# A decode step on one core: cached pages loaded four rows to a partition, turned by VectorE, scored in 32x32 array tiles

## The chip, the cores and the metric

The kernel runs on one core of one Trainium2 chip. The metric is the device time of one execution in microseconds (us). TensorE (PE) multiplies matrices, VectorE (DVE) and ScalarE (ACT) work element by element, GpSimd (POOL) and SyncE (SP) mostly issue transfers. Each engine runs its own list of instructions in order, and semaphores tie the lists together. SBUF has 128 partitions; matrix products land in eight PSUM banks of 128 x 512 fp32.

## The reference

Two layers; layer 0 is the one that matters. A prompt of 512 tokens and 8 sequences of 4 new tokens go through multi-head latent attention. Each sequence has 4096 cached positions in 32 pages, found through a page table; a page is 128 rows of 320 fp32 (256 latent, 64 rotary key), 160 KB. For a sequence, with 8 heads x 4 tokens = 32 queries:

```python
q_lat = jnp.einsum('bthd,chd->bthc', q_nope, w_uk)
s_past = (jnp.einsum('bthc,bkc->bhtk', q_lat, c_past).astype(jnp.float32)
          + jnp.einsum('bthr,bkr->bhtk', q_rope, kr_past).astype(jnp.float32)) * MLA_SCALE
...
p = jax.nn.softmax(jnp.concatenate([s_past, s_new], axis=-1), axis=-1).astype(c.dtype)
o_lat = (jnp.einsum('bhtk,bkc->bthc', p[..., :past_len], c_past)
         + jnp.einsum('bhtk,bkc->bthc', p[..., past_len:], c))
```

Then come the up-projection by `w_uv`, the output projection by `mla_wo`, a mixture of experts (32 experts, 6 MB of weights each), and layer 1 (sliding-window attention, experts again). All in fp32.

## The kernel before

The part that changes is the sampled stage of layer 0, from about 216 us (absorbing `w_uk` into the queries) to 405.7 us (the last values). It runs over the sequences b = 0..7, and each sequence in quarters t = 0..3 of 8 pages.

**Pages.** `pages[b % 2]` are two buffers of a whole sequence (40 KB a partition each). Page j of a sequence lies in all 128 partitions, 1280 bytes (one row) in each, at column block j. POOL loads sequences 0 and 1 early (L620 to L631), between 65 and 163 us. From b = 2 on, SP loads quarters 0 and 2 (L449 to L461), POOL quarters 1 and 3 (L635 to L645), each page by one DMA. They wait for the values of sequence b-2, which free the buffer piecewise: `page_mm` counts after i = 1, 3 and 5 of the values' loop, `pv_mm` after its end.

**TensorE** for a quarter (`keys_T`, `scores`): 20 transposes of 128x128 (`flip`, L2021) turn the 8 pages' rows into columns, in PSUM banks 2 to 6. ACT copies banks 2, 4 and 6 to SBUF (through a helper at L752), DVE banks 3 and 5 (L1324). Then 12 products score the keys against the 32 queries: weights of 32 columns, four column tiles of the array at a time, 256 keys each, in banks 0 and 1. A product of fp32 (helper `mm`, L2016) shows as two matmul records, a flip as one.

**The softmax.** DVE takes the maximum over bank 0 (L1329, L1331) and bank 1 (L1336), and L1338 makes the negative scaled maximum (semaphore `nms_ready`). ACT's `weigh` takes the exponentials in two halves (L923, L926) and of the new keys (L928). `weights_T` turns the 128x1024 weights back in 8 + 1 flips; ACT and DVE (L1345, L1347) copy them out. `values` is 33 products with four column tiles in bank 7, whose right-hand sides are the page rows themselves.

The order on TensorE is written out by hand: keys_T(b,0), scores(b-1,3), keys_T(b,1), scores(b,0), weights_T(b-1), values(b-1), keys_T(b,2), scores(b,1), keys_T(b,3), scores(b,2). So the softmax of a sequence runs beside the transposes of the next.

After values(6), SP loads `mla_wo` (L493), 4 MB, which the output projection needs right after values(7). `w_uk` and `w_uv` come as one tensor `wkvb`, loaded at 197.4 us.

## Time and profile before

| | |
|---|---|
| median of three runs | 1846.52 us (1845.17 to 1849.54) |
| span of the profiled execution | 1842.6 us |
| TensorE busy | 1743.9 us (95%) |
| VectorE, ScalarE, GpSimd busy | 602.8, 381.9, 214.1 us |
| values of sequence 0 and 7 start at | 253.79 and 399.96 us |
| one sequence (TensorE busy, VectorE busy) | 21.3 us (20.99, 7.96) |

The profiled execution has no time of its own beside its span; the median of the runs is 3.9 us above the span. "Clock" in a stretch is the granted clock of TensorE as a share of 2.4 GHz, so that 0.50 is 1.2 GHz. A row of the groups gives the line, engine, operation and shape, the count, the busy time, the mean of one in ns, then the idle time just before them and who ended it.

### The profile page before, as it was taken

The numbers are of one execution on the slowest core, as the hardware profiler recorded it, in microseconds if no ns is written. First come the engines' busy times: TensorE is split into PE (matmuls) and PEld (weight loads), VectorE is DVE, ScalarE is ACT, GpSimd is POOL, SyncE is SP. The second block draws the span as 40 slices with busy tenths as digits, with TensorE's granted clock in tenths as the row PEclk, the third lists the DMA queues.
The fourth block names the chain that finished last, engine by engine and source line by source line (L and its number), as shares of the span: only waits on it lengthen the run. The fifth ranks groups of instructions, "written<-read, shape, count | busy, mean of one in ns | idle before, by whom it ended". The sixth has DMA issues, their size and how long they took to land.

```text
span 1842.6 us, 29042 instructions
## 1 busy us (share of the span) xinstructions
PE 1743.9 (95%) x9946; PEld 871.1 (47%) x9947; DVE 602.8 (33%) x1586; ACT 381.9 (21%) x858; POOL 214.1 (12%) x312
## 2 busy tenths in 40 slices
PE   7899899999899999999999899999899999999995
PEld 5466676655544444434344445455444444333342
DVE  2334343331522222222222556764322222212223
ACT  2233344431111111111011224342011111111112
POOL 1231014410001000000010201000000010000010
PEclk9899999999989999999999999999899999999998
DMA  6252137775449999999998800032899999999974
GB/s 181 68 155 88 50 116 237 254 253 208 159 182 404 414 421 417 412 419 419 415 418 350 303 14 1 20 138 85 347 375 412 422 414 418 414 421 408 418 307 151
DMA packets 80624, 511.63 MB, mean 278 GB/s; under 512 B 20917, under 2 KB 39302, under 8 KB 54074
## 3 DMA queue, kind: packets, MB, share of 16 engines
q1 hardware_dynamic: 61962, 461.35, 62.1%
q0 software_dynamic: 18576, 49.16, 8.1%
q8 instruction: 51, 0.84, 0.2%
q14 instruction: 35, 0.29, 0.1%
HBM read 498.07 MB, written 26.52 MB: 285 GB/s over the span
## 4 chain that ended last, share of the span: by engine, by line
PE 75%; DMA 14%; DVE 5%; issue 2%; ACT 2%; DVEq 1%; SPq 0%; POOL 0%; ACTq 0%; POOLq 0%
PE ps L2016 65%; DMA mem<-in_moe_w_up 11%; PE ps L2021 10%; ACT mem L752 1%; DMA mem<-in_x_sample 1%; DMA mem<-in_c_masks 1%; DVE mem L1794 0%; DMA mem<-moe_rows_back 0%; DMA mem<-in_cache_mla 0%; DMA moe_rows_back<-mem 0%; DVE mem L1765 0%; DMA mem<-in_swa_sinks 0%; DVE mem L1336 0%; ACT mem L923 0%; ACT mem L926 0%
## 5 line engine op out<-in xcount | busy, mean ns | idle before, releaser
L2016 PE MATMUL ps<-mem 128*64 128x512 f32 (+14 forms) x7970 | 1510.1, 485 | 62.2 <-DMA mem<-moe_rows_back 14.0
L2016 PEld LDWEIGHTS ps<-mem 128*64 128x64 f32 (+4 forms) x7970 | 641.9, 145 | 837.8 <-issue 747.6
L752 ACT ACTIVATE mem<-ps 128x512 f32<-128x512 f32 (+4 forms) x370 | 205.7, 567 | 621.9 <-PE ps L2016 425.2
L2021 PE MATMUL ps<-mem 128*128 128x128 f32 (+1 forms) x1976 | 274.8, 280 | 28.9 <-DMA mem<-in_x_prompt 6.9
L2021 PEld LDWEIGHTS ps<-mem 128*128 128x128 f32 (+1 forms) x1976 | 234.2, 171 | 125.0 <-issue 101.7
L1636 DVE TENSOR_TENSOR mem<-mem,ps 64x512 f32<-64x512 f32 x64 | 44.2, 690 | 433.2 <-ACT mem L995 433.2
L692 POOL DMA_INDIRECT moe_rows_back<-mem x64 | 57.3, 896 | 853.5 <-DVE mem L1653 842.6
L995 ACT ACTIVATE mem<-ps 64x512 f32<-64x512 f32 x64 | 37.7, 589 | 557.8 <-PE ps L2016 557.8
L1653 DVE COPY mem<-ps 64x512 f32<-64x512 f32 x64 | 44.4, 693 | 147.2 <-PE ps L2016 147.2
L1324 DVE COPY mem<-ps 128x512 f32<-128x512 f32 x64 | 44.2, 692 | 77.0 <-PE ps L2021 73.0
L644 POOL DMA_DIRECT2D mem<-in_cache_mla x96 | 51.7, 538 | 104.2 <-PE ps L2016 94.2
L1617 DVE COPY mem<-ps 64x512 f32<-64x512 f32 x32 | 22.2, 694 | 89.4 <-PE ps L2016 89.4
L624 POOL DMA_DIRECT2D mem<-in_cache_mla x64 | 34.4, 538 | 114.1 <-issue 114.1
L1062 ACT ACTIVATE mem<-mem 128x256 f32<-128x256 f32 (+1 forms) x64 | 30.3, 474 | 61.6 <-DVEq L1799 61.6
L682 POOL DMA_INDIRECT mem<-moe_rows_in,mem x34 | 33.2, 977 | 79.3 <-issue 79.3
L1794 DVE CUSTOM_DVE_ANT_0 mem<-ps,mem 128x256 f32<-128x256 f32 (+1 forms) x64 | 26.3, 448 | 27.2 <-PE ps L2016 25.1
L1561 DVE TENSOR_TENSOR mem<-mem 128x320 f32<-128x320 f32 x70 | 34.0, 486 | 2.1
L665 POOL DMA_DIRECT2D moe_rows_in<-mem x10 | 5.4, 538 | 237.8 <-DVE mem L1452 237.8
L1720 DVE SCALAR_TENSOR_TENSOR mem<-mem 128x1024 f32<-128x1024 f32 (+1 forms) x16 | 23.1, 1441 | 23.1 <-DMA mem<-moe_rows_back 21.8
L1644 DVE COPY mem<-ps 128x256 f32<-128x256 f32 x64 | 27.2, 425 | 8.1
L867 ACT ACTIVATE mem<-mem 128x128 f32<-128x128 f32 (+3 forms) x32 | 18.0, 561 | 37.8 <-DVEq L1273 37.8
L1622 DVE TENSOR_TENSOR mem<-ps,mem 128x512 f32<-128x512 f32 x32 | 22.1, 692 | 9.8 <-PE ps L2021 9.7
(237 smaller groups left out, 485.2 us busy)
## 6 DMA issues: line engine op xcount, KB each, us to landing
mem<-in_moe_w_gate SPq DMA_DIRECT2D x64, 2048.0 KB, 21.3
mem<-in_moe_w_up SPq DMA_DIRECT2D x64, 2048.0 KB, 27.8
mem<-in_moe_w_down SPq DMA_DIRECT2D x64, 2048.0 KB, 19.4
mem<-in_cache_mla POOLq DMA_DIRECT2D x160, 160.0 KB, 4.4
mem<-in_cache_mla SPq DMA_DIRECT2D x96, 160.0 KB, 5.5
mem<-moe_rows_back SPq DMA_DIRECT2D x8, 1024.0 KB, 8.7
mem<-in_mla_wo SPq DMA_DIRECT2D x1, 4096.0 KB, 14.1
moe_rows_in<-mem POOLq DMA_DIRECT2D x8, 512.0 KB, 3.0
```

What stands on the lines that cost most here:

```text
L624: g.dma_start(pages_flat[par][:, bass.ds(j * ROW, ROW)], a["cache_mla"][0][bass.ds(page, 1)].rearrange("a p c -> p (a c)")).then_inc(sig[f ...
L644: g.dma_start(pages[b % 2][:, j, :], a["cache_mla"][0][bass.ds(at[n], 1)].rearrange("a p c -> p (a c)")).then_inc(sig[f"late_pages{b % 2}" ...
L682: g.indirect_dma_start(out=xe[b][0:BLK, :], out_offset=None, in_=rows_in, in_offset=bass.IndirectOffsetOnAxis(ap=fetch_at[b][0:BLK, 0:1].b ...
L692: g.indirect_dma_start(out=rows_back, out_offset=bass.IndirectOffsetOnAxis(ap=store_at[b][0:BLK, 0:1].bitcast(U32), axis=0), in_=ye[b][0:B ...
L752: return act.activation(out, in_, ACT.Copy)
L995: act.activation(sg[BLK:2 * BLK, :], ps[0:BLK, b, :], ACT.Silu).then_inc(sig["silu_ready"], 1)
L1324: v.tensor_copy(kT[t % 2][:, n], ps[:, bank, :].rearrange("p (g c) -> p g c", g=2)).then_inc(sig[f"tp_ev{bank}"], 1)
L1561: v.tensor_tensor(onehot[b], rankm[:, :, cols(q, 1)].broadcast_to([P, TILES, BLK]), slots.unsqueeze(1).broadcast_to([P, TILES, BLK]), ALU. ...
L1636: v.tensor_tensor(hid[0:BLK, :], sg[BLK:2 * BLK, :], ps[BLK:2 * BLK, b, :], ALU.mult).then_inc(sig["hid_ready"], 1)
L1653: v.tensor_copy(ye[b][0:BLK, FF:D], ps[BLK:2 * BLK, 2 + b, :]).then_inc(sig["y1_ready"], 1)
L2016: return pe.matmul(out, lhsT, rhs, start=start, stop=stop)
L2021: return pe.transpose(out, in_, ident[at:at + n, at:at + n])
```

## The change

**Loads.** A page now goes to 32 partitions: four consecutive rows (5120 B) to a partition. Page j goes to partitions 32*(j%4) and up, at column block j//4 (of four rows' width). The number of DMAs, their issuers and what they wait for stay.

**Transposes.** The 80 flips of a sequence, and their copies, go. VectorE turns the page buffer in 32x32 blocks straight from SBUF to SBUF: four `transpose` of 128 x 2560 a sequence, into `keysT[0]` and `keysT[1]` (one for each half of the sequence). `keysT` is not double-buffered: keys_T(b,0) waits for the first half of the scores of b-1.

**Scores.** Each 32x32 block is a right-hand side for a 32-row array tile. The queries must lie in every group of 32 partitions: ten products with the selector `pick` spread them (`qrep`), once. A half is 10 (j) x 4 (row tiles i, one PSUM bank each) x 4 (column tiles g) products of 32x32 weights with 128 columns, so 320 a sequence.

**Softmax.** One maximum over 4 banks x 256 (L1327); the exponentials read and write in strides that put the weights back into the pages' order. ACT makes all three copies of `weights_T`. `values` is the same but for its indices.

**Order and the rest.** TensorE now runs weights_T(b-1), values(b-1), scores(b,0), scores(b,1). VectorE runs keys_T(b,0), largest(b-1), keys_T(b,1), (b,2), (b,3). `w_uk` and `w_uv` are loaded by two DMAs each, `w_uv` after the last scores; a load of the last expert's down weights waits for `oc_mm`; one POOL load of the norm's gain waits for the last `weights_T`, as the softmax weights now lie in its place. Buffers are placed anew.

```diff
@@ loads (SP; POOL alike)
-                    sp.dma_start(pages[b % 2][:, j, :], a["cache_mla"][0][bass.ds(at[n], 1)].rearrange("a p c -> p (a c)")
+                    sp.dma_start(four_rows(b % 2, j // 4 * 4 * ROW, j % 4), page_rows(at[n])).then_inc(...)
+        def page_rows(page):
+            return a["cache_mla"][0][bass.ds(page, 1)].rearrange("a (p s) c -> p (a s c)", s=4)
+        def four_rows(par, at, i):
+            return pages_flat[par][32 * i:32 * (i + 1), cols(at, 4 * ROW)]
@@ SP, after values(6)
             sp.dma_start(wo_m, a["mla_wo"][0].rearrange("(k p) n -> p k n", p=P)).then_inc(sig["wo_in"], DMA)
+            sp.wait_ge(sig["qk_mm"], happened("qk_mm", 2 * NB))
+            for k in range(2):
+                sp.dma_start(wuv[:, k], wkv_heads[:, k, :, 1, :]).then_inc(sig["wkvb_in"], DMA)
@@ VectorE
+            def keys_T(b, n):
+                if b < 2 and n == 0:
+                    v.wait_ge(sig[f"late_pages{b % 2}"], landed(f"late_pages{b % 2}", PAGES))
+                if b >= 2:
+                    name, before_ = (("pages", 0), ("late_pages", PAGES), ("third_pages", 0), ("fourth_pages", 0))[n]
+                    v.wait_ge(sig[f"{name}{b % 2}"], landed(f"{name}{b % 2}", before_ + QUARTER * (b // 2)))
+                if n % 2 == 0:
+                    v.wait_ge(sig["qk_mm"], happened("qk_mm", max(2 * (b - 1) + n // 2 + 1, 0)))
+                v.transpose(keysT[n // 2][:, n % 2 * QUARTER * ROW:(n % 2 + 1) * QUARTER * ROW],
+                            pages_flat[b % 2][:, n * QUARTER * ROW:(n + 1) * QUARTER * ROW]).then_inc(sig["keysT_ready"], 1)
+            def largest(b):
+                v.wait_ge(sig["qk_mm"], happened("qk_mm", 2 * b + 2))
+                v.tensor_reduce(m_s[:, b:b + 1], ps[:, 0:4, 0:2 * P], XY, ALU.max)
...
+            keys_T(0, 0)
+            keys_T(0, 1)
             for n in range(1, 4, 2):
                 v.wait_ge(sig["wuk_mm"], happened("wuk_mm", n + 1))
...
+            keys_T(0, 2)
+            for n in range(1, 5, 2):
+                v.wait_ge(sig["qrep_mm"], happened("qrep_mm", n + 1))
+                v.tensor_copy(qrep[:, 2 * n:2 * n + 2], ...)
+            keys_T(0, 3)
...
+            for b in range(1, NB):
+                keys_T(b, 0)
+                largest(b - 1)
+                for n in range(1, 4):
+                    keys_T(b, n)
@@ TensorE
+            for j in range(ROW // 32):
+                rows, q = (slice(0, P), qlat[:, j // 4]) if j < 8 else (slice(0, DR), qmix[0:DR])
+                last = mm(ps[:, j // 2, ...], pick[rows, j % 4, :], q.rearrange("p b q -> p (b q)"), True, True)
+            def scores(b, half_):
+                if half_ == 0:
+                    pe.wait_ge(sig["p_s_ready"], happened("p_s_ready", 2 * b))
+                pe.wait_ge(sig["keysT_ready"], happened("keysT_ready", 4 * b + 2 * half_ + 2))
...
+                for j in range(ROW // 32):
+                    for i in range(4):
+                        for g in range(4):
+                            last = mm(ps[g * NS:(g + 1) * NS, i, c0:c0 + P].rearrange("p (m k) -> p m k", m=4),
+                                      qrep[rows, j, b, :], blocks[rows, :, g, 32 * j:32 * (j + 1)], j == 0, j == ROW // 32 - 1)
```

TensorE's list before, from the end of keys_T(2,1) over scores(2,0) to the first flips of weights_T(1):

```order
L2021 MATMUL ps<-mem 128x128 [waits tp_ev6]
L2021 MATMUL ps<-mem 128x128 x3
L2016 MATMUL ps<-mem 32x256 [waits tp_ev3,tp_ev2,p_s_ready]
L2016 MATMUL ps<-mem 32x256 x3
L2016 MATMUL ps<-mem 32x256 [waits tp_ev5,tp_ev4]
L2016 MATMUL ps<-mem 32x256 x3
L2016 MATMUL ps<-mem 32x256 [waits tp_ev6]
L2016 MATMUL ps<-mem 32x256 x3
L2021 MATMUL ps<-mem 128x128 [waits tp_ev2,p_s_ready]
L2021 MATMUL ps<-mem 128x128 x3
```

and TensorE's list for one whole sequence after (L2013 is `mm` now, L2018 is `flip`):

```order
L2018 MATMUL ps<-mem 128x128 [waits pT_s_ready,p_s_ready]
L2018 MATMUL ps<-mem 128x128 x3
L2018 MATMUL ps<-mem 32x32 [waits pTn_ready]
L2013 MATMUL ps<-mem 32x256 [waits pT_s_ready,o_s_ready]
L2013 MATMUL ps<-mem 32x256 x15
L2013 MATMUL ps<-mem 32x256 [waits pT_s_ready]
L2013 MATMUL ps<-mem 32x256 x15
L2013 MATMUL ps<-mem 32x256 [waits pTn_ready]
L2013 MATMUL ps<-mem 32x128 [waits keysT_ready,p_s_ready]
L2013 MATMUL ps<-mem 32x128 x159
L2013 MATMUL ps<-mem 32x128 [waits keysT_ready]
L2013 MATMUL ps<-mem 32x128 x159
```

The flips and their copies' semaphores (`tp_ev2` to `tp_ev6`) are gone from between the scores, and between scores(b,1) and values(b) nothing else stands any more but the softmax's own flips.

VectorE's list before, keys_T(1,0), the maximum of sequence 0, keys_T(1,1) and a copy of weights_T(0) (the same for later sequences):

```order
L1324 COPY mem<-ps 128x512 [waits tp_mm3,qk_mm]
L1324 COPY mem<-ps 128x512 [waits tp_mm5]
L1336 TENSOR_REDUCE mem<-ps 128x1 [waits qk_mm]
L1338 TENSOR_SCALAR mem<-mem 128x1
L1324 COPY mem<-ps 128x512 [waits tp_mm3,qk_mm]
L1324 COPY mem<-ps 128x512 [waits tp_mm5]
L1345 COPY mem<-ps 128x512 [waits pv_mm,tp_mm3]
```

and after, from keys_T(2,0) with the maximum of sequence 1 behind it:

```order
L1321 STREAM_TRANSPOSE mem<-mem 128x2560 [waits qk_mm,pages0]
L1327 TENSOR_REDUCE mem<-ps 128x1 [waits qk_mm]
L1329 TENSOR_SCALAR mem<-mem 128x1
L1321 STREAM_TRANSPOSE mem<-mem 128x2560 [waits late_pages0]
L1321 STREAM_TRANSPOSE mem<-mem 128x2560 [waits qk_mm,w_a_in]
L1321 STREAM_TRANSPOSE mem<-mem 128x2560 [waits consts_in]
```

The wait for landed pages (`pages0` and so on; `w_a_in` and `consts_in` are the semaphores that the third and the fourth quarter of these buffers share by the table `LATER`) has moved from TensorE to VectorE, and stands ahead of the maximum (L1327) of the sequence before.

## Rows read from the trace of the kernel before

**Rows 1.** Busy time and chain of waits: parts 1 and 4 of the page.
```profile
PE 1743.9 (95%) x9946; PEld 871.1 (47%) x9947; DVE 602.8 (33%) x1586; ACT 381.9 (21%) x858; POOL 214.1 (12%) x312
...
PE 75%; DMA 14%; DVE 5%; issue 2%; ACT 2%; DVEq 1%; SPq 0%; POOL 0%; ACTq 0%; POOLq 0%
```

**Rows 2.** Busy time by stretch: window, length, PE, PEld, DVE, ACT, POOL, clock, DMA share, GB/s.
```profile
228.50:253.80 25.30, 24.99 (x251) 18.86 (x251) 12.11 (x26) 12.72 (x25) 0.00 (x0) 0.92 0.00 1
258.00:279.30 21.30, 20.99 (x252) 14.40 (x253) 7.96 (x14) 9.68 (x20) 8.32 (x17) 1.00 0.75 248
...
399.90:403.30 3.40, 3.34 (x32) 1.80 (x36) 2.73 (x17) 0.00 (x0) 0.00 (x0) 0.51 0.00 0
222.40:228.50 6.10, 3.84 (x17) 3.47 (x16) 2.07 (x7) 1.14 (x3) 0.00 (x0) 0.50 0.01 3
228.50:232.70 4.20, 4.20 (x21) 4.18 (x21) 1.15 (x2) 1.20 (x2) 0.00 (x0) 0.50 0.00 0
```

**Rows 3.** Chain that ends last, start of the sampled stage: start, length, what.
```profile
219.15 4.02 PE ps L2016 x32
...
225.42 3.18 PE ps L2016 x12
228.59 6.53 PE ps L2021 x40
235.12 1.57 PE ps L2016 x24
...
253.79 4.21 PE ps L2016 x66
```

**Rows 4.** Groups by shape, one period, 258 to 279.3 us.
```profile
L2021 PE MATMUL ps<-mem 128*128 128x128 f32 x89 | 11.0, 276 | 0.0
...
L1324 DVE COPY mem<-ps 128x512 f32<-128x512 f32 x8 | 5.5, 692 | 9.4 <-PE ps L2021 8.9
```

**Rows 5.** Timeline, last sequence: start, length, what, idle before and its releaser.
```profile
395.76 0.69 DVE L1336 TENSOR_REDUCE mem<-ps 128x1 f32<-128x512 f32 x1 [2.09 <-PE ps L2016]
...
399.22 0.60 ACT L752 ACTIVATE mem<-ps 128x512 f32<-128x512 f32 x1 [0.16 <-issue]
...
399.96 0.65 PE L2016 MATMUL ps<-mem 128*32 128x256 f32 x4 [0.36 <-ACT mem L752]
```

**Rows 6.** Chain of waits from 400 us.
```profile
399.96 30.22 PE ps L2016 x146
```

**Rows 7.** VectorE groups by shape, longer rows.
```profile
L1452 DVE SCALAR_TENSOR_TENSOR mem<-mem 128x1024 f32<-128x1024 f32 x8 | 10.3, 1285 | 1.0 <-issue 0.4
...
L1914 DVE TENSOR_TENSOR mem<-mem 128x1280 f32<-128x1280 f32 x1 | 1.5, 1484 | 0.0
```

**Rows 8.** Array tiles of 64 rows and 32 columns, later in the program: groups, then the window.
```profile
L2016 PEld LDWEIGHTS ps<-mem 64*32 64x32 f32 x128 | 3.6, 136 | 0.7 <-issue 0.7
...
1196.00:1199.60 3.60, 3.60 (x130) 3.59 (x128) 2.00 (x9) 1.19 (x5) 0.00 (x0) 0.63 0.54 138
```

**Rows 9.** SP's page issues after the first values: start, length, count.
```profile
255.08 7.47 SPq L460 DMA_DIRECT2D mem<-in_cache_mla  x12
```

**Rows 10.** Page transfers: first 10 us of a burst, one period, the early ones.
```profile
DMA packets 1857, 3.39 MB, mean 339 GB/s; under 512 B 318, under 2 KB 1490, under 8 KB 1856
...
mem<-in_cache_mla SPq DMA_DIRECT2D x17, 160.0 KB, 6.2
...
mem<-in_cache_mla POOLq DMA_DIRECT2D x64, 160.0 KB, 2.5
```

**Rows 11.** Chain around 305 us.
```profile
305.81 7.01 DMA mem<-in_cache_mla
```

**Rows 12.** VectorE before the first wuk copy.
```profile
217.44 0.69 DVE L1305 COPY mem<-ps 128x512 f32<-128x512 f32 x1 [4.95 <-PE ps L2021]
```

**Rows 13.** The transfers to 32 partitions and of mla_wo.
```profile
mem<-in_x_sample SPq DMA_DIRECT2D x1, 128.0 KB, 16.5
...
mem<-in_mla_wo SPq DMA_DIRECT2D x1, 4096.0 KB, 14.1
```

More of the change, by code:

```diff
@@ L11 @@
 X = mybir.AxisListType.X
+XY = mybir.AxisListType.XY
 P = 128
@@ L25 @@
 PAGES = 32
+HALF, QUARTER = PAGES // 2, PAGES // 4
 PHYS = 320
@@ L284, in build, with pair_buffers @@
         ptab = m.take(NB * PAGES, dt=I32)
+        samples_from = m.at
+        def pair_buffers():
+            return m.take(SEQ), [m.take(SEQ) for _ in range(2)], [m.take(SEQ) for _ in range(2)], m.take(PT, 2 * DN)
+        qsw = m.take(TOK)
+        even_pair = pair_buffers()
         cosT = m.take(TOK)
         sinT = m.take(TOK)
-        pair_from = m.at
         wqp = m.take(3, 2 * (DN + DR))
@@ L320, in build @@
         pn = over.take(NB, NS)
-        pTn = s.take(NS)
-        mn, m_s, m2_s, nm_s, l_s, l2_s, ln_s, w_s = (s.take(NB) for _ in range(8))
-        mg, lg_s, dg = (s.take(4, NB) for _ in range(3))
-        mt, lt_s = (s.take(NB) for _ in range(2))
-        assert s.at <= WORDS - 2 * 2 * H * DN and qsw.shape[1] == TOK
-        wkvb = Arena(mem, WORDS - 2 * 2 * H * DN, WORDS).take(2, 2 * H * DN)
         r = Arena(mem, work, moe_end)
@@ L941, in values @@
                 copy(o_s[:, b, :], ps[:, 7, 0:CL]).then_inc(sig["o_s_ready"], 1)
-            for b in range(NB):
-                keys_T(b, 0)
-                if b:
-                    weigh(b - 1)
-                keys_T(b, 1)
-                if b:
-                    weights_T(b - 1)
-                    values(b - 1)
-                keys_T(b, 2)
-                keys_T(b, 3)
+            for b in range(NB - 1):
+                weigh(b)
+                weights_T(b)
+                values(b)
             weigh(NB - 1)
@@ L2240, in weights_T @@
-                pe.wait_ge(sig["tp_ev6"], happened("tp_ev6", at))
-                flip(ps[0:NS, 6, 0:NS], pn[0:NS, b, :]).then_inc(sig["tp_mm6"], 1)
+                        last = flip(ps[:, 4 + half_, i * P:(i + 1) * P], p_s[:, (4 * half_ + i) * P:(4 * half_ + i + 1) * P])
+                    last.then_inc(sig["pT_s_mm"], 1)
+                pe.wait_ge(sig["pTn_ready"], happened("pTn_ready", b))
+                flip(ps[0:NS, 6, 0:NS], pn[0:NS, b, :]).then_inc(sig["pTn_mm"], 1)
             def values(b):
-                page, at = pages[b % 2], weights_at(b)
+                page = pages[b % 2]
@@ L2274, in _ @@
                     values(b - 1)
-                keys_T(b, 2)
+                scores(b, 0)
                 scores(b, 1)
-                keys_T(b, 3)
-                scores(b, 2)
-            scores(NB - 1, 3)
             weights_T(NB - 1)
```

236 lines of the change are left out of this document (90 added, 146 removed).

## The prediction, made before the changed kernel ran

> **What bounds the kernel now.** I read the page first. TensorE is busy for 1743.9 us of the 1842.6 us span, and the chain that ends last is 75% TensorE against 5% VectorE [rows 1]. So what TensorE no longer does is gained, if nothing else gets in the way. Next the windows of the stage that changes: in one sequence's period of 21.3 us TensorE is busy for 20.99, VectorE for 7.96, ScalarE for 9.68 at clock 1.00, and the transfer engines 75% of it [rows 2]. The chain of waits agrees: from 228.59 on it is TensorE alone (flips 6.53, scores 1.57, flips 2.33, and so on, values 4.21 at 253.79) [rows 3]. The groups of one period say what TensorE does: 89 flips fill 11.0 us of it [rows 4]. The stage has three marks that I use below: values(0) start at 253.79 [rows 3], values(7) at 399.96 [rows 5], and from there the chain is TensorE without a gap for 30.22 us [rows 6]. So the seven periods between take 146.2 us, and what values(7) start earlier the program ends earlier, as long as the weights behind it have landed.
>
> **The change part by part.** It takes 80 flips a sequence from TensorE and gives it nothing to hide the softmax behind. The new length P of a period, from values to values, is the longest of three loops.
>
> *TensorE's loop:* values 4.2 us (66 records) [rows 3], then the scores S, then the wait for the softmax. In the last sequence, where that wait already stands bare, the maximum starts at 395.76 and the values at 399.96: 4.2 us [rows 5]. The new maximum reads 1024 elements instead of 512. VectorE's mean is 1285 ns for 1024 elements and 1484 for 1280, against 0.69 us for the 512 of the maximum [rows 5, 7]; so it costs 0.5 us more, and the wait becomes 4.7. The two exponentials keep their size; I cost their strides at nothing (up to 0.7 us if they halve their rate, 0.69 each now [rows 5]).
>
> *The price of the scores* isn't in the trace, since no sixteen tiles run there. 24 records of 256 columns on four tiles take 1.57 us [rows 3], 262 ns for a round of four, so 131 ns for 128 columns. The change issues 320 products, 640 records. If sixteen run at once, that is 40 rounds, S = 5.2 us; if eight, 10.5; if four, 21. A second bound is the rate of starts: later in the program, 128 pairs of weight load and product on tiles of 64 rows by 32 columns take 3.6 us at a mean clock of 0.63 [rows 8], 28 ns each, in a stretch that also streams. 640 of them would take 18 us, or 11.3 if all of it scales with the clock. Both ends are kept. I take 6.5, near the streaming bound, since the four column tiles in [rows 3] already overlap fully: a round of four takes 262 ns, little over what one matmul of the group does alone (276 ns for a flip [rows 4]). TensorE's loop is then 4.2 + 0.3 (change of tile shape) + 6.5 + 0.1 + 4.7 = 15.8 us, at full clock.
>
> *The clock.* In before the bare wait of 4.2 us was followed by 3.4 us at 0.51, from 399.9 on [rows 2, 5], the lower of the two levels (1.2 and 2.4 GHz): 1.7 us more for the values. The change puts such a wait, of 4.7 us or more, into each period. I charge 1.7 us each time: the loop is 17.5.
>
> The Trainium skill, "TensorEngine Tiling (Array Packing)" and "TensorE: Matmul & The Clock Gate" (Part 3), has sixteen 32x32 tiles 10.6 times faster than one after the other, with starts 4 ns apart. By that S would stay at its streaming bound; no run here shows it yet.
>
> *VectorE's loop:* a transpose of 2560 elements isn't in the trace. From 512 elements at 0.69 us and 1280 at 1.48 [rows 5, 7] one element costs 1.03 ns, so 2.8 us; at half that rate it is 5.5. Four a sequence, plus 1.2 and 0.2 for the maximum: 12.8 us (23.6 at half rate). I take the full rate, as every two-operand row of VectorE shown has it. The 8 copies that go (5.5 us [rows 4]) were hidden and return nothing.
>
> *The pages' loop* is the longest. The wait for pages now stands on VectorE, ahead of the maximum of the sequence before. Quarter 0 of b can load only once the values of b-2 are past i = 1. In before, values(0) start at 253.79 and SP's first page is issued at 255.08, twelve of them in 7.47 us [rows 9], so the eighth about 4.4 later, 5.7 after the values' start. Landing takes 2.5 us for a page that has the engines to itself and 6.2 in a burst [rows 10], 7.0 in the chain at 305.81 [rows 11]; I take 5.5, since the same DMAs are issued by the same queues. A quarter of the values (1.0 us) comes before i = 1 is done, 2.0 at half clock, so quarter 0 is there 12.2 us after the values' start. Then keys_T(b,0) 2.8, a gap of 0.1 and the softmax 4.7 give P = 19.8. With 2.5 for the landing the pages' loop is 16.8, with 7.0 it is 21.3. Behind it are three more transposes, done 1.4 + 8.6 = 10.0 us after the maximum's start, while the values run from 4.7 to 10.6 and the first half of the scores to 14.1, so they are hidden.
>
> The bytes: a burst moves 339 GB/s in its first 10 us [rows 10], so 5.24 MB a sequence take 15.5 us, within 19.8.
>
> *The start.* VectorE has 4.95 us free before its copy at 217.44 [rows 12]; two transposes of b = 0 (5.6, plus gaps) fill it and push the copies and the product behind them by about 0.7. From the end of that product (219.15 + 4.02 [rows 3], now 223.9) copies lead to 224.4. The ten `qrep` products come in a stretch at clock 0.50, from 222.4 to 232.7 [rows 2]. One is two records of 256 columns: 0.52 us at full clock by the 262 ns above, 0.95 to 1.05 at half. They end at about 233. The twelve records of new keys (3.18 at half clock [rows 3]) take 1.6 at full: 234.6. Scores(0) end at 241.2, where keys_T(1,0) and the small work on the new keys are done (about 240.8), and values(0) start at 246.0, 7.8 earlier.
>
> *The sum.* From values(0): six periods of 19.8 and a last one of 17.5, since no pages stand before the last maximum, are 136.3. Values(7) start at 246.0 + 136.3 = 382.3 instead of 399.96: 17.7 us less. The `mla_wo` load takes 14.1 us to landing [rows 13] from the end of values(6), so it lands 14.1 + 5.9 - 17.5 = 2.5 after the start of values(7), which take 4.2 to 5.9 us: hidden by 1.7 us at least. `w_uv`, 1 MB behind it, is needed only after two output projections. The rest of the program I take as it is. The executions stand 3.9 us above the span, so the median 1846.5 becomes 1829.
>
> **The likeliest case and its ends.** If the landings are short and the clock stays up, all periods are 15.8: 246.0 + 110.6 = 356.6, 43.4 less, 1803. If the scores take 10.5 (values(0) 4 us later, periods of 21.5), values(7) start at 400.5, 1847. This case holds 0.56.
>
> **Rival 1: half of the write paths (slower, 0.14).** All 128 partitions took each page before, now 32. If the transfer engines share the way into those 32, a sequence takes up to 31 us. Then the stage is one stream: values(7) = 246 + 1 + 6T + 12, which passes 399.96 at T = 23.5. Midway, T = 27: 421, 21 us more, 1868; at 31, 1891. For it: the one load to 32 partitions, `x_sample` of 128 KB, takes 16.5 us to land [rows 13]; against it: that is at the start of the program, behind 2 MB of others, and several pages for different quadrants are under way at once.
> The Trainium skill, "SBUF — State Buffer" (Door 1, and "Can I just issue two DMAs to hit both halves?"), states that partitions 0 to 31 are reached by 8 of 16 ports, at 189 GB/s for 1 MiB, and that two transfers at once gain 6%. By its 189 to 200 GB/s a sequence would take 26 to 28 us, about the midway price. No row shows it for pages, as each engine's share is the same before and after.
>
> **Rival 2: starts bound the scores (slower, 0.12).** From S = 10.4 on (values(7) = 239.5 + 77 + 8S, where TensorE's loop is the longest) the change loses. The unscaled 18 us of [rows 8] give 460.5, 60 more, 1907; 12 us give 1859. For it: 1280 TensorE instructions a sequence for products of 128 columns, each hardly longer than its weight load. Against: the overlap in [rows 3].
>
> **Rival 3: VectorE turns at half rate (slower, 0.08).** A period is 23.6 plus gaps, 24.2, and the start is 8 us later: 254 + 6 x 24.2 + 17 = 416, 16 more, 1862. It decides from about 4.9 us for a transpose.
>
> **Rival 4: the clock stays down (slower, 0.10).** If TensorE ran at 1.2 GHz through whole periods, values would take 8.4 and the scores 13: periods of 27.3, values(7) at 437, 37 more, 1884. It decides from about 6 us of lost work a period (P = 22). For it: the drop at 222.4 lasted until 232.7 [rows 2], 10 us, with TensorE working without a gap from 225.4 [rows 3]. Against: the one at 399.9 lasted 3.4.
>
> **That it changes nothing (0.05 to 0.06)** needs a period near 21.8, which eats the 7.8 us of the start: a landing of 7.5 us does that.
>
> **The numbers.** A measurement of this kernel tells changes from about 0.2% (3.7 us) on. Faster: 0.52 of the likeliest's 0.56, and 0.05 from the others' near ends: 0.57. The same 0.06, slower 0.37. The likeliest case's own range is 1803 to 1847; 8 in 10 is 1803 to 1872, leaving out the far ends of rivals 1, 2 and 4.
>
> **What the changed profile would show.** Right: `STREAM_TRANSPOSE` 128x2560 at 2.8 us; the 320 products of a sequence in 5 to 8 us; values 19 to 20 us apart, in some of them the clock at 0.5, VectorE idle before the transpose that waits for the first quarter; pages landing in 5 to 6 us; a gap of 4 us and more on TensorE between scores and values; values(0) at 246. Wrong: landings above 8 us with TensorE waiting on pages (rival 1); a TensorE busy without gaps for over 12 us in the scores (rival 2); a VectorE above 90% busy in the stage (rival 3); an output projection that waits for `in_mla_wo`; a clock of 0.5 through whole periods (rival 4). The largest danger to the number is the landing of the first quarter: each microsecond of it counts six times.

## The result, and the profile after

The changed kernel takes 1964.39 us (median; 1957.31 to 1966.64), the kernel before 1845.85 us beside it: ratio 1.064, 95% interval 1.062 to 1.067. It is 6% slower; I had forecast 1829 us and faster, and the time lies outside the range up to 1872.

The span is 1955.7 us, 113.1 more than before. The marks of the prediction say where. Values(0) start at 256.15, which was 253.79 [rows 3]; values(7) start at 516.4, which was 399.96 [rows 5]. So the start of the stage gave nothing back (2.4 us later, forecast 7.8 earlier), and the seven periods take 260.3 us instead of 146.2: 37.2 us each instead of 20.9, forecast 19.8. The rest of the program took 3 us less. Where "the 119 us" stand below, they are the 118.5 us between the two medians.

The page, parts 1, 2 (clock) and 3 (queues) of the kernel after:

```profile
PE 1738.5 (89%) x13678; PEld 869.2 (44%) x13679; DVE 638.6 (33%) x1522; ACT 333.2 (17%) x779; POOL 206.7 (11%) x312
...
PEclk9899866666798999999999999999999999999997
...
q8 instruction: 80, 1.31, 0.3%
```

TensorE has 3732 records more than in [rows 1] and is yet busy for 5 us less. Its granted clock is at 0.6 to 0.7 in the slices of the stage. And a queue that nobody looks at first: the page has 80 packets of 16 KB of TensorE's instructions (51 before).

One period, TensorE's timeline, kernel after (start, length, engine, line, what, count, and in brackets the idle time before it and who ended it; "issue" is nobody that the profile shows):

```profile
256.15 7.45 PE L2013 MATMUL ps<-mem 128*32 128x256 f32 x242
268.48 2.81 PE L2013 MATMUL ps<-mem 32*32 32x128 f32 x128 [4.88 <-issue]
278.24 2.84 PE L2013 MATMUL ps<-mem 32*32 32x128 f32 x128 [6.95 <-issue]
285.25 2.82 PE L2013 MATMUL ps<-mem 32*32 32x128 f32 x128 [4.18 <-issue]
288.71 2.04 PE L2013 MATMUL ps<-mem 32*32 32x128 f32 x80 [0.64 <-issue]
293.19 2.45 PE L2018 MATMUL ps<-mem 128*128 128x128 f32 x9 [2.45 <-ACTq L936]
295.57 1.94 PE L2013 MATMUL ps<-mem 128*32 128x256 f32 x16
```

This is the view that gives it away. The first row holds the 66 records of the values and the first 176 of the scores. After them the scores run in pieces of exactly 128 records, each with its weight load: 256 instructions. A piece takes 2.8 us; the stops before the pieces take 4.88, 6.95, 4.18 and 0.64 us, 16.7 us in all, and no engine or transfer of data ends them. The softmax, bare as forecast, is the 4.8 us from 290.76 to 295.57.

Over the whole stage (256 to 520 us) the stops of this kind are 28, four in each of the seven periods, and take 101 of the 114 us by which the stage grew (who waited for whom: us in total, times, the longest):

```profile
PE ps L2013 <- issue: 101.1, 28, 6.9
```

The trace also has the packets of the instruction queue, q8. In this period there are six. In the stop from 271.29 to 278.24 none is under way until 275.30; then comes one (row of the queue from 275.30 to 276.72: packets, MB, share of 16 engines):

```profile
q8 instruction: 1, 0.02, 6.1%
```

The next piece of 128 records starts 1.5 us behind it. So one packet arrives for each piece, which makes 256 instructions to 16 KB.

The windows of the same period (window, length, PE, PEld, DVE, ACT, POOL, clock, DMA share, GB/s):

```profile
270.00:274.00 4.00, 1.29 (x62) 0.78 (x53) 0.00 (x0) 0.00 (x0) 0.00 (x0) 0.50 1.03 213
274.00:278.00 4.00, 0.00 (x0) 0.00 (x0) 0.00 (x0) 0.00 (x0) 0.00 (x0) 0.50 1.04 224
278.00:282.00 4.00, 2.84 (x128) 2.15 (x128) 2.85 (x1) 0.00 (x0) 0.00 (x0) 0.50 1.02 221
290.00:294.00 4.00, 1.55 (x36) 0.98 (x16) 3.14 (x3) 1.56 (x5) 0.00 (x0) 0.50 0.00 0
```

From 274 to 278 no engine works: only the transfers do, all sixteen engines busy (1.04) at 224 GB/s, where a burst moved 339 before [rows 10]. TensorE's clock is at 0.50. The long stops fall in the page traffic; after it, at 288, the stop is 0.64.

And the two things that I had priced well: the transpose, and who waits for pages.

```profile
L1321 DVE STREAM_TRANSPOSE mem<-mem 128x2560 f32<-128x2560 f32 x32 | 89.2, 2822 | 89.0 <-PE ps L2013 79.1
```

A transpose takes 2.82 us (2.8 forecast), and VectorE waits for TensorE, not for pages.

### The profile page after: what moved, and what is told of

Same layout as the page of the kernel before. It is cut to its first block, busy times and chain, and to the rows that moved or that the text cites. A ratio compares the mean times of both kernels' runs of the same rounds, so it can differ in the third digit from the quotient of the medians.

```text
span 1955.7 us, 36123 instructions
## 1 busy us (share of the span) xinstructions
PE 1738.5 (89%) x13678; PEld 869.2 (44%) x13679; DVE 638.6 (33%) x1522; ACT 333.2 (17%) x779; POOL 206.7 (11%) x312
## 4 chain that ended last, share of the span: by engine, by line
PE 72%; DMA 13%; issue 7%; DVE 5%; ACT 1%; DVEq 1%; SPq 0%; ACTq 0%; POOLq 0%
PE ps L2013 65%; DMA mem<-in_moe_w_up 12%; PE ps L2018 7%; ACT mem L932 1%; DVE mem L1327 1%; DVE mem L1791 0%; DMA mem<-in_mla_w_a 0%; DMA mem<-moe_rows_back 0%; DVE mem L1762 0%; DMA mem<-in_mla_wq_b 0%; DVE mem L1754 0%; DVE mem L1755 0%; ACT mem L764 0%; DMA moe_rows_back<-mem 0%; DVE mem L1808 0%
## 5 line engine op out<-in xcount | busy, mean ns | idle before, releaser
L2013 PE MATMUL ps<-mem 32*32 32x128 f32 (+12 forms) x12342 | 1569.8, 446 | 161.9 <-issue 111.2
L2013 PEld LDWEIGHTS ps<-mem 32*32 32x32 f32 (+5 forms) x12342 | 706.0, 140 | 942.4 <-issue 862.6
L764 ACT ACTIVATE mem<-ps 128x512 f32<-128x512 f32 (+5 forms) x291 | 157.0, 548 | 589.8 <-PE ps L2013 435.9
L2018 PE MATMUL ps<-mem 64*128 64x64 f32 (+4 forms) x1336 | 206.1, 289 | 47.8 <-ACTq L936 19.8
L2018 PEld LDWEIGHTS ps<-mem 64*128 64x128 f32 (+4 forms) x1336 | 168.3, 189 | 135.4 <-issue 92.1
L1321 DVE STREAM_TRANSPOSE mem<-mem 128x2560 f32<-128x2560 f32 x32 | 89.2, 2822 | 89.0 <-PE ps L2013 79.1
L655 POOL DMA_DIRECT2D mem<-in_cache_mla x96 | 47.0, 490 | 190.7 <-PE ps L2013 177.5
L932 ACT ACTIVATE mem<-ps,mem 128x512 f32<-128x512 f32 x16 | 11.0, 688 | 217.8 <-DVE mem L1329 217.0
L636 POOL DMA_DIRECT2D mem<-in_cache_mla x64 | 31.6, 494 | 106.0 <-issue 106.0
L1327 DVE TENSOR_REDUCE mem<-ps 128x1 f32<-128x1024 f32 x8 | 9.8, 1225 | 97.3 <-PE ps L2013 97.3
L1791 DVE CUSTOM_DVE_ANT_0 mem<-ps,mem 128x256 f32<-128x256 f32 (+1 forms) x64 | 26.3, 449 | 27.6 <-PE ps L2013 25.1
## 6 DMA issues: line engine op xcount, KB each, us to landing
mem<-in_moe_w_gate SPq DMA_DIRECT2D x64, 2048.0 KB, 21.2
```

The source lines that it names most:

```text
L636: g.dma_start(four_rows(par, block_ * (4 * ROW), i), page_rows(page)).then_inc(sig[f"late_pages{par}"], DMA)
L655: g.dma_start(four_rows(b % 2, j // 4 * 4 * ROW, j % 4), page_rows(at[n])).then_inc(sig[f"late_pages{b % 2}" if n < 8 else f"fourth_pages{ ...
L764: return act.activation(out, in_, ACT.Copy)
L1321: v.transpose(keysT[n // 2][:, n % 2 * QUARTER * ROW:(n % 2 + 1) * QUARTER * ROW], pages_flat[b % 2][:, n * QUARTER * ROW:(n + 1) * QUARTE ...
L2013: return pe.matmul(out, lhsT, rhs, start=start, stop=stop)
L2018: return pe.transpose(out, in_, ident[at:at + n, at:at + n])
```

## The experiments

Three theories. **A**: TensorE waits for its own instructions; a block of 256 has to be fetched every 128 small products, and the fetch stands behind the page traffic. **B**: pages to 32 partitions come at two thirds of the rate, and pace the stage. **C**: the starts of small products, about 20 ns a pair, set the scores. Below, the hardware loops that repeat one group are there to take the instructions away; what they leave out stands in their expectations.

**Fewer bytes (e2).** Of each page a twentieth:

```diff
-sp.dma_start(four_rows(b % 2, j // 4 * 4 * ROW, j % 4), page_rows(at[n]))
+sp.dma_start(four_rows(b % 2, j // 4 * 4 * ROW, j % 4)[:, 0:64], page_rows(at[n])[:, 0:64])
```
(POOL alike.)

> The changed kernel, but of each page of b >= 2 only 256 of the 5120 bytes of each partition are loaded (the rest of the keys is what lay there): same number of transfers, a twentieth of the bytes. Theory A: the stops between blocks of 128 products fall from 4 to 7 us to the 0.7 to 1.1 us seen in scores(0), so a sequence's scores take 5 x 3.5 = 17 us instead of 28 to 30 and the period 27 to 29 us: 1895 to 1905. Theory B: the period falls by what the pages paced; since VectorE waits only 9.8 us in all for pages, little by itself. Theory C (the start rate of small products sets the scores): no change, 1960 or more.

Measured: 1895.04 us, ratio 1.027 (1.024 to 1.031). Its TensorE in one period:

```profile
283.23 7.87 PE L2013 MATMUL ps<-mem 128*32 128x256 f32 x293
292.86 1.92 PE L2013 MATMUL ps<-mem 32*32 32x128 f32 x128 [1.76 <-issue]
296.59 2.81 PE L2013 MATMUL ps<-mem 32*32 32x128 f32 x128 [1.81 <-issue]
300.31 2.81 PE L2013 MATMUL ps<-mem 32*32 32x128 f32 x128 [0.92 <-issue]
304.04 0.73 PE L2013 MATMUL ps<-mem 32*32 32x128 f32 x29 [0.92 <-issue]
```

The same pieces of 128, the stops now 0.6 to 1.8 us. The period is 26 to 28 us, but for the last. There the 4 MB of `mla_wo` are loaded beside the scores, and the stops are long again, 4.63 and 3.73 us:

```profile
431.29 2.74 PE L2013 MATMUL ps<-mem 32*32 32x128 f32 x128 [4.63 <-issue]
```

So 69 us of the 119 go with the bytes of the pages; the stops themselves stay without them.

This run also shows what the clock does to a piece. Two pieces of the period above, the first and the third (columns as in the windows before):

```profile
292.86:294.78 1.92, 1.92 (x128) 1.57 (x128) 0.36 (x1) 0.00 (x0) 1.62 (x4) 1.00 0.19 38
300.31:303.12 2.81, 2.81 (x128) 2.14 (x128) 0.00 (x0) 0.00 (x0) 0.00 (x0) 0.50 0.03 6
```

The same 128 records take 1.92 us at clock 1.00, 15 ns each, and 2.81 at 0.50, 22 ns each. In the changed kernel all pieces behind the first stop of the period shown ran at 0.50.

**Fewer instructions (e3).** The middle of the scores as a loop:

```diff
-                for j in range(ROW // 32):
-                    (16 products of group j)
+                sixteen(0, True, False)
+                with pe.Fori(1, ROW // 32 - 1) as j:
+                    sixteen(1, False, False)
+                last = sixteen(ROW // 32 - 1, False, True)
```

> The changed kernel, but of a half's ten groups of sixteen products the eight in the middle are a hardware loop of one and the same group (j = 1 eight times, so j = 2 to 8 are left out of the sums): as many products of the same size, a fifth to a quarter of the instructions to be fetched. Pages as in the changed kernel. Theory A: the stops go; 640 pairs at the 19 to 22 ns within a block take 12 to 14 us, and the period falls to what pages allow at 215 GB/s (24 to 25 us): 1870 to 1885. Theory C (starts alone, or something in the 32x32 tiles): stops or a low rate remain, 1940 or more.

Measured: 1858.11 us, ratio 1.008 (1.006 to 1.010), better than expected. In the first three periods no piece is left: values and scores are one run of TensorE, and what waits now is the softmax, for VectorE, which waits for pages. From the fourth period on single stops come back, the longest 3.53, 4.44 and 3.43 us; the last row is one. The instructions outside the small loops still have to be fetched, which would explain them, but that is not tested here.

```profile
276.50 16.17 PE L2013 MATMUL ps<-mem 128*32 128x256 f32 x706
297.37 2.46 PE L2018 MATMUL ps<-mem 128*128 128x128 f32 x9 [4.71 <-ACTq L936]
299.76 14.75 PE L2013 MATMUL ps<-mem 128*32 128x256 f32 x706
321.70 2.45 PE L2018 MATMUL ps<-mem 128*128 128x128 f32 x9 [7.19 <-ACTq L936]
...
344.55 0.64 PE L2013 MATMUL ps<-mem 32*32 32x128 f32 x6 [3.53 <-issue]
```

```profile
DVE mem L1321 <- DMA mem<-in_cache_mla: 58.7, 15, 8.4
```

Theory A holds: with page traffic as in the changed kernel (232 GB/s in its row below) and the same number and size of products, 106 of the 119 us are gone. Theory C has its part: within the scores, at clock 1.00, 513 records take 8.00 us (262 to 270 us), 15.6 ns each, so 640 take about 10 us and not the 5.2 of streaming.

**Half of the instructions (e5).** 160 products of 256 columns:

```diff
-last = mm(ps[g * NS:(g + 1) * NS, i, c0:c0 + P].rearrange("p (m k) -> p m k", m=4),
-          qrep[rows, j, b, :], blocks[rows, :, g, 32 * j:32 * (j + 1)], ...)
+last = mm(ps[g * NS:(g + 1) * NS, i, 0:2 * P].rearrange("p (h m k) -> p h m k", h=2, m=4),
+          qrep[rows, j, b, :], blocks[rows, :, :, g, 32 * j:32 * (j + 1)], ...)
```

> The changed kernel with 160 products of 256 columns a sequence instead of 320 of 128 (both halves of the keys in one right-hand side): same columns streamed, half the instructions; keys_T(b,0) now waits for all the scores of b-1. Theory A: 2.5 blocks instead of 5 a sequence, half of the stops: scores 12 to 15 us, period 25 to 28, 1885 to 1900. Theory C (each start costs 20 ns): scores fall by 6 us, 1915 to 1925. Theory D (streaming bounds the scores): no change or 10 us slower from the lost overlap.

Measured: 1887.79 us, ratio 1.024 (1.021 to 1.027). As theory A had it; neither C alone (1915 and more) nor D. The edit halves the starts as well as the instructions to be fetched, so by itself it does not part A from C; the size of the gain does.

**The page rate: rotated (e1), alone (e4), undone (e6).** e1 moves POOL's pages two quadrants on:

```diff
-g.dma_start(four_rows(b % 2, j // 4 * 4 * ROW, j % 4), page_rows(at[n]))
+g.dma_start(four_rows(b % 2, j // 4 * 4 * ROW, (j + 2) % 4), page_rows(at[n]))
```

> The changed kernel (1964 us) with one edit: POOL's pages of b >= 2 go two quadrants of partitions further than SP's, so that the two queues do not fill the same 32 or 64 partitions at a time; any order of pages gives the same sums. Theory A (TensorE waits for its own instructions, whose 16 KB blocks queue behind the page traffic): it gains only as far as the page traffic gets shorter. Theory B (32 partitions take a page at half the width, 215 GB/s against 339 before, and the pages pace the stage): the rate rises to above 300 GB/s, packets of 5120 B fall from 355 to below 260 ns and the periods of 37.3 us fall by 8 us or more, 1905 us or less. If two queues in different halves do not help, nothing changes: 215 GB/s and 1960 to 1968.

Measured: 1957.66 us, ratio 1.061 (1.058 to 1.065). The rate moved little (260, 229, 265 and 228 GB/s in four windows, against 229, 236, 214 and 223), so the edit is no cure (the time is not clear of the changed kernel's own spread), and it says nothing on theory B's size.

e4 puts only the loads of the change into the kernel before:

```diff
-sp.dma_start(pages[b % 2][:, j, :], a["cache_mla"][0][bass.ds(at[n], 1)].rearrange("a p c -> p (a c)"))
+sp.dma_start(four_rows(b % 2, j // 4 * 4 * ROW, j % 4), page_rows(at[n]))
```

> The kernel before with the loads alone changed: pages of b >= 2 go to 32 partitions, four rows each; all its flips and products stay (a page's rows then lie in other places than its code takes them for, which changes which key is weighed by what). Theory B (the 32 partitions halve the page rate whatever the rest does): packets of 5120 B take 350 us-thousandths (ns) and more, a sequence's 5.24 MB take 24 us, and TensorE, which needed 21.3 us, now waits for pages: periods of 24 to 26 us from the third on, 1860 to 1875. If the low rate came from something in the changed kernel's compute, or if half of the width did not matter here, 1843 to 1848.

Measured: 1862.53 us, ratio 1.010 (1.005 to 1.015). The flips now wait for pages, 20.1 us in all, where the same wait took 2.3 us in the kernel before:

```profile
PEld ps L2029 <- DMA mem<-in_cache_mla: 20.1, 12, 4.4
```

So theory B is true as to the rate, and worth 18 us in a kernel that is quick enough to notice. e6 is the other way round, the changed kernel with the old loads (the diff of e4 reversed):

> The changed kernel with the loads alone undone: each page of b >= 2 goes to all 128 partitions (1280 B each), as before; VectorE's transposes and the 320 products stay (the sums are the same, keys in another order). Theory A with B: page traffic runs at 340 GB/s or more and lasts 15 instead of 24 us of each period, so one or two blocks fewer of the five meet it: stops of 4 to 7 us become 0.7 to 1 there, the period falls from 37.3 to 29 to 33 us, 1905 to 1935. Theory A without B (the stops depend on there being page bytes, not on the rate): 1955 or more. The floor is the run with few page bytes, 1895.

Measured: 1927.11 us, ratio 1.045 (1.039 to 1.051). POOL's packets of 5120 B are back at 219 ns (from 355), and one period reads:

```profile
289.23 8.71 PE L2013 MATMUL ps<-mem 128*32 128x256 f32 x293
301.87 2.52 PE L2013 MATMUL ps<-mem 32*32 32x128 f32 x128 [3.92 <-issue]
308.34 2.81 PE L2013 MATMUL ps<-mem 32*32 32x128 f32 x128 [3.95 <-issue]
312.34 2.80 PE L2013 MATMUL ps<-mem 32*32 32x128 f32 x128 [1.20 <-issue]
315.79 0.73 PE L2013 MATMUL ps<-mem 32*32 32x128 f32 x29 [0.65 <-issue]
```

Two long stops instead of three, and 4 us instead of 4 to 7: 37 us of the 119. The narrow loads hurt by keeping the traffic on longer, in which instructions come late.

**Both, and the limits (e7, e8, e9).** e7 is e6 with e5's products, e8 is e6 with e3's loop, e9 has all three.

> Wide loads and 160 products of 256 columns together. Theory A: half of the blocks and a shorter traffic; scores 12 to 13 us, wait and softmax 5, values 4.2, 1.7 for the clock: period 23 to 25, 1862 to 1875. If the two do not add up, it stays near the better of the two alone (1888).

Measured: 1871.74 us, ratio 1.015 (1.008 to 1.022). Together the two save 93 us of the 119; alone they save 77 (e5) and 37 (e6), 114 in sum. Most of it adds up, not all: both shorten the same stops.

> Wide loads and the hardware loop in the scores (j = 1 eight times, j = 2 to 8 left out), so neither the fetch nor the page rate stands in the way. What is left is the start rate: 640 pairs at 19 ns are 12.2 us, values 4.2, softmax 4.8: periods of 21.3 to 22, 1835 to 1845, no faster than before. If TensorE could start the sixteen tiles as fast as they stream (5.2 us), the period would be 16 to 17 and the time 1805 to 1815.

Measured: 1847.6 us, ratio 1.001 (0.999 to 1.003): neither faster nor slower than the kernel before, and just above the expected range, with periods of 20.7 to 22.5 us. Fetch and page rate away, the 320 small products are worth just what the 80 flips and 48 products were. TensorE's row is 15.88 us for 706 records. It holds the values too, 5.2 us of it at a mean clock of 0.66. The second row is scores(0) alone, without page traffic (columns as in the windows before):

```profile
297.58 15.88 PE L2013 MATMUL ps<-mem 128*32 128x256 f32 x706
...
240.05:250.21 10.16, 10.16 (x641) 6.33 (x640) 5.31 (x11) 0.00 (x0) 0.00 (x0) 1.00 0.01 2
```

So 640 records take 10.2 us at clock 1.00, 15.9 ns each. The 19 ns of the expectations mix both clocks: in the changed kernel the piece from 240.06 on takes 2.48 us, at a mean clock of 0.65.

> Wide loads, 160 products of 256 columns and the hardware loop (j = 1 eight times, j = 2 to 8 left out): the columns that the changed kernel streams, half of its starts, no stops for instructions. If a start (19 ns a pair) set the scores in the last loop run (12.2 us), they take about 6.4 us now, and with 4.2 + 1.5 for the values, 2.8 for the transpose that no longer overlaps and 4.8 for the softmax the period is 19.5 to 20.5: 1825 to 1835, faster than before. If streaming set them (the sixteen tiles not being all at work at once), they stay at 12 us and the time is 1860 to 1870.

Measured: 1834.03 us, ratio 0.996 (0.993 to 0.998), the one run that was faster than the kernel before, by 0.4%, with seven of ten groups replaced by repeats of another. Its scores have a row of their own:

```profile
304.81 6.53 PE L2016 MATMUL ps<-mem 32*32 32x256 f32 x320 [1.00 <-DVE mem L1324]
316.61 2.45 PE L2021 MATMUL ps<-mem 128*128 128x128 f32 x9 [5.27 <-ACTq L939]
```

320 records in 6.53 us are 20.4 ns each, at twice the columns. The 640 of e8 took 10.2 us or more, 15.9 ns each. The same columns in half as many records are 3.6 us quicker, so at 128 columns the number of products sets the time, as theory C said: S is 10.2 and up, not 6.5. At 256 columns it is not the number alone: 320 at 15.9 ns would be 5.1 us, streaming 5.2, and 6.53 it was. What adds the rest is open. That the expectation of 6.4 was met is luck, since it rested on 19 ns.

**The clock (e10), and the transpose ahead of the maximum (e11).** Into e7, in the wait for the softmax:

```diff
+                    for _ in range(5):
+                        mm(ps[:, 4, :], ident, x[0:P, 0:FF], True, True)
                     weights_T(b - 1)
```

> Wide loads and 160 products of 256 columns, unrolled (1872 us), with five products of 128x512 into a free bank put between the scores and the softmax's flips, where TensorE waits 5.3 us anyway: about 4.3 us of work at full clock that no one reads. If the half clock after each wait costs what it seems (1.5 us in the values and up to 1.7 us in the flips, exchange and scores), the period falls by 1.5 to 3 us and the time to 1850 to 1862. If the clock does not matter, or the filler is in the way: 1872 or more.

Measured: 1872.24 us, ratio 1.015 (1.011 to 1.020), not the 1850 to 1862 expected.

```profile
318.92 8.01 PE L2016 MATMUL ps<-mem 32*32 32x256 f32 x18 [1.94 <-issue]
326.76 1.17 PE L2021 MATMUL ps<-mem 128*128 128x128 f32 x9
328.20 4.20 PE L2016 MATMUL ps<-mem 128*32 128x256 f32 x66 [0.27 <-ACT mem L767]
```

The filler does hold the clock for what follows (flips 1.17 instead of 2.45 us, values 4.20). But behind the scores' stops the clock was already at 0.50 (from 312.40 on), and the filler (with the last scores 8.01 us) ran at it until 323.5, past the end of the wait. e11 also puts `largest(b - 1)` ahead of `keys_T(b, 0)`:

> The last one with the maximum of b-1 ahead of keys_T(b,0) on VectorE, which the transpose delays by 2.8 us. The four transposes then end 12.8 us after the scores instead of 11.4, and the scores of b could start 10 us after. One gain of 2.8, one new wait of 2 to 3 us for keysT: the same within 5 us of the last one. If the transposes are hidden by the values and the filler, 15 to 20 us faster.

Measured: 1867.38 us, ratio 1.013 (1.008 to 1.018), 5 us below e10: as expected.

**The whole computation without the fetch (e12).** This is e7 (wide loads, 160 products of 256 columns) with TensorE's list over the sequences as a hardware loop of three turns, two sequences each, some 1600 instructions a turn; ScalarE copies the queries of the next sequence to one fixed place:

```diff
+            scores(0)
+            with pe.Fori(0, NB // 2 - 1) as pair:
+                for par in range(2):
+                    b = pair * 2 + par
+                    weights_T(b)
+                    values(b, par)
+                    scores(b + 1, False)
+            weights_T(NB - 2)
...
@@ ScalarE, after weights_T(b)
+                copy(qb, qrep[:, :, b + 1, :]).then_inc(sig["qrep_act"], 1)
```

> [...] If the some 1600 instructions of a turn stay on the engine, no block is fetched in turns 2 and 3: periods of about 28 us in turn 1 and 20.5 in turns 2 and 3, 1843 to 1852; with the first turn as slow as before it is about the same as the kernel before. If the turn is too long to stay, all periods are 24 to 28 and the time is 1868 to 1880.

Measured: 1848.83 us, ratio 1.002 (1.000 to 1.004). Turn 1, then turn 2, then a row of the last scores, behind the loop:

```profile
277.62 10.15 PE L2020 MATMUL ps<-mem 128*32 128x256 f32 x284
290.23 3.56 PE L2020 MATMUL ps<-mem 32*32 32x256 f32 x102 [2.46 <-issue]
299.12 2.43 PE L2025 MATMUL ps<-mem 128*128 128x128 f32 x9 [5.33 <-ACTq L940]
301.48 12.11 PE L2020 MATMUL ps<-mem 128*32 128x256 f32 x386
318.95 2.43 PE L2025 MATMUL ps<-mem 128*128 128x128 f32 x9 [5.36 <-ACTq L940]
...
396.42 4.00 PE L2020 MATMUL ps<-mem 32*32 32x256 f32 x115 [3.37 <-issue]
```

The queues of the 60 us of turns 2 and 3 (there is no q8 any more, where the 49 us before them have a row `q8 instruction: 6`):

```profile
q1 hardware_dynamic: 6904, 7.86, 41.3%
q0 software_dynamic: 2301, 7.87, 38.2%
q14 instruction: 4, 0.03, 0.1%
```

Turn 1 has periods of 25.1 and 23.9 us and its stops. In turns 2 and 3 the same instructions, under the same traffic, run without one, and the periods are 19.8 to 21.0. The last scores stand behind the loop, as instructions of their own, and there a stop of 3.37 us is back (last row). Nothing is left out of the sums here, so this shows theory A in a kernel that does the whole work.

**Which partitions (e13).** e3 with the queues kept apart:

```diff
-                mine = [HALF * i + j for i in range(2) for j in range(QUARTER)]      # SP
+                mine = [4 * (n // 2) + n % 2 for n in range(16)]
-                mine = [16 * i + 8 + j for i in range(2) for j in range(8)]           # POOL
+                mine = [4 * (n // 2) + 2 + n % 2 for n in range(16)]
```

> The changed kernel with narrow loads and the loop in the scores (1858 us; j = 1 eight times, j = 2 to 8 left out), but SP loads only the pages of partitions 0 to 63 and POOL only those of 64 to 127, both from the first quarter on. Theory B1 (what halves the rate is that the partitions in use at a time share their way in, 0 to 63 one half and 64 to 127 the other): the rate rises from 230 GB/s to over 300, packets of 5120 B fall to below 270 ns, and the time to 1845 to 1850, where the wide loads with the same loop are. Theory B2 (each transfer to 32 partitions is slow by itself, whoever else runs): 220 to 250 GB/s and 1855 to 1865.

Measured: 1857.76 us, ratio 1.008 (1.006 to 1.010). The windows of e3 and of e13:

```profile
300.00:315.00 15.00, 14.51 (x706) 8.49 (x698) 6.09 (x3) 0.75 (x3) 7.84 (x16) 0.97 1.00 232
```

```profile
300.00:310.00 10.00, 9.96 (x518) 5.92 (x510) 3.74 (x2) 0.38 (x1) 7.11 (x15) 0.97 1.01 268
```

232 GB/s became 268 here; over the stage it is 222 to 247 in four windows of e3 and 247 to 312 in five of e13, and the median packet takes 294 to 299 ns instead of 367. That is between B1 (over 300 GB/s) and B2 (up to 250), and no time came of it, since keys_T(b,0) now waits for both queues. It shows that which partitions are filled at the same time has a part in the rate; it leaves open what the rest is.

**Clock and fetch away (e15, e16).** e10's filler, five products, in e12; e16 with three of them and the maximum ahead of keys_T(b,0).

> The last kernel (b-loop on TensorE, whole computation, 1848.8 us) with five products of 128x512 into a free bank, that no one reads, in the 5.4 us in which TensorE waits for the softmax. If the clock that is at 0.5 after each such wait is a cost of its own, values fall from 6.1 to 4.2 us, the nine flips and their copies from 2.4 to 1.5: periods of 17.5 to 18.5 in turns 2 and 3, 1828 to 1836, faster than before. If the clock does not go by that, or the filler runs over the end of the wait, 1848 or more.

> The same with three of the five products and the maximum of b-1 ahead of keys_T(b,0), which ends the wait 2.8 us earlier: values could start at 16 us a period, but four transposes (11.3) and the maximum (1.4) then stand between the scores of b-1 and those of b, so a period is at least 12.8 + 6.5 = 19.3. Slower than the last one by 5 to 10 us, if that chain is the longest; otherwise faster by as much.

Measured: 1848.84 us, ratio 1.002 (1.000 to 1.004), and 1849.3 us, ratio 1.003 (1.001 to 1.004). Neither gained anything over e12: the 1828 to 1836 expected of e15 did not come, and e16 was neither slower nor faster than e15. The filler does its part in e15, and it is lost right behind it:

```profile
318.95 8.29 DVE L1328 STREAM_TRANSPOSE mem<-mem 128x2560 f32<-128x2560 f32 x3
...
321.88 4.20 PE L2020 MATMUL ps<-mem 128*32 128x256 f32 x66
...
327.48 12.41 PE L2020 MATMUL ps<-mem 32*32 32x256 f32 x330 [1.40 <-DVE mem L1328]
335.54 2.85 DVE L1328 STREAM_TRANSPOSE mem<-mem 128x2560 f32<-128x2560 f32 x1 [8.30 <-PE ps L2020]
```

Values are back at 4.20 us (6.07 in e12), but then the scores wait 1.40 us for the last transpose (4.12 in e16, where the transposes start later). With one buffer for the turned keys and all of them in each product, the four transposes (11.1 us), the maximum (1.4) and the scores (6.5) add up to one chain of 19.0 us a sequence, and the periods of the loop in e15 are 19.4 to 21.2. No version computed all and beat the kernel before.

## Why the prediction was wrong

**The step that failed is the price of the scores.** I took S = 6.5 us, near the 5.2 us of streaming on sixteen tiles. Measured in the first full period: 640 records run for 13.7 us (3.2 + 2.81 + 2.84 + 2.82 + 2.04) and stop for 16.7, S = 30.4. Three things are in it:

- *The starts*, a term that I had too small. At clock 1.00 the 640 records take 10.2 us (scores(0) of e8), 15.9 ns each, where I counted on 6.5. The mistake was in what I took from [rows 3]. Four column tiles of 256 columns fully overlap in 262 ns a round, and I went on from there to sixteen tiles of 128 columns. But a round of four hides four starts of 16 ns behind 262 ns of columns; a round of sixteen has 131 ns for sixteen. The row that was nearer in kind, [rows 8], gave 11.3 us with the clock taken out. I had kept it as an end only. The starts 4 ns apart that the prediction quotes beside its sum are not what these runs show at 128 columns: 15 to 16 ns.
- *The wait for instructions*, a term that I had put at nothing: 16.7 us of this period and 101 us of the seven (e2, e3, e12).
- *The half clock inside the scores.* I had charged it to the values alone. Behind the first stop the pieces take 22 ns a record instead of 15, about 3.5 us of the 13.7 by e2's two rows.

**Rival 2 was the right one, for the smaller part of its reason.** It said that starts bound the scores and that the change loses from S = 10.4 on. With nothing but the starts left (e8) the change neither wins nor loses, as its formula has it for 10.4. For S = 18 it gave 1907, and the rest of the way to 1964 was not in it. It counted 1280 TensorE instructions a sequence, and stopped there. The kernel before has about two packets of instructions in a period of 21.3 us; I knew none of their cost, because nothing waited for them. The changed kernel needs five to six in a period. The counter that I should have priced is on the page: `q8 instruction: 51` before, 80 after.

The Trainium skill, "Runtime: NRT & Kernel Launch" (Instruction fetch mechanics), states that instructions come in blocks of 16 KB, that TensorE holds eight of them, and that crossing into the next is mostly hidden. The first is as the trace has it (one 16 KB packet to a piece of 128 pairs). The second agrees with e12, where a turn of some 1600 instructions is not fetched again; no run here tries a longer loop. The third does not hold here: 0.6 to 1.8 us a block without page traffic, up to 7 us with it.

**Rival 1 came true as a rate and did not decide.** 213 to 224 GB/s with all transfer engines busy; a sequence's pages took 24 us, near the 23.5 from which it would decide. In the changed kernel VectorE waited 9.8 us in all for pages; the lower rate alone costs 18 us (e4), behind the loop 10.5 (e3 against e8). What it cost in the changed kernel, 37 us (e6), went by a way that the rival did not name: the traffic lasts longer, and more instructions arrive in it. The Trainium skill, "SBUF — State Buffer" (Door 1), gives 189 GB/s at 1 MiB and about 218 at most for partitions 0 to 31; the 213 to 224 GB/s here, with several transfers to different quadrants under way, lie at its upper figure. Its section "Can I just issue two DMAs to hit both halves?" has two transfers at once only 6% above one. No run here compares one with two; with many under way, sorting the two queues by halves gave 15% in one window (232 to 268 GB/s, e13).

**Rival 3 fell**: 2.82 us a transpose. **Rival 4** was half right: the clock was at 0.50 not only after the softmax but behind the long stops in the scores too, 0.63 on average from 256 to 516. What it costs is seen in e15 for the values (4.20 us instead of 6.07; my 1.7 us were about right) and in e2 for a piece of the scores (1.92 us instead of 2.81).

**The pages' loop**: the first quarter was to land 12.2 us after the values' start. In e8, where nothing else is slow, keys_T(b,0) starts 11.6 us after them (276.5, 288.1). Right, but it paced nothing in the changed kernel. The forecast of 4.7 us for the softmax was 4.8.

**The start**: 7.8 us to be gained from the first flips were lost to the same things; scores(0), without any page traffic, took from 235 to 251.3, 16 us instead of 6.5. In e8, without the fetch, it took 10.2.

## What to carry to other kernels

Before replacing few large TensorE instructions by many small ones, count the instructions, not only the columns: here a pair (weight load and product) of a 32x32 tile with 128 columns started every 15 to 16 ns at clock 1.00 and every 22 at 0.50, and every 128 pairs a block of instructions had to arrive, at 0.6 to 1.8 us a stop in a quiet stretch and up to 7 us behind transfers. Read the clock beside each row before taking a rate from it. Read the instruction queue's row as one reads the others, and look for rows of equal count with "issue" before them. A gap that an engine's work used to cover has to be priced with what then becomes longest: three times here (pages, clock, transposes) a gain went straight into the next wait.

## What the runs showed of the hardware

- TensorE's instructions travel as 16 KB packets on a queue of their own (q8), one for each 128 pairs, and arrive late while pages are loaded. With that traffic cut to a twentieth, the stops fell from as much as 4 to 7 us to 0.6 to 1.8 (e2); in a hardware loop of some 1600 instructions they were gone from the second turn on (e12).
- An fp32 pair on 32x32 tiles takes 15 to 16 ns at 128 columns and 20.4 at 256 at clock 1.00 (e2, e8, e9), and 22 ns at 128 columns at clock 0.50 (e2).
- Pages to 32 partitions each move at 213 to 236 GB/s in the changed kernel, the packet of 5120 B taking 355 ns instead of 219; two queues in different halves of the partitions reach 247 to 312 (e13).
- VectorE's transpose of 128x2560 fp32 in 32x32 blocks takes 2.82 us, 1.1 ns a column.
